# Attention scores as rounded products over 128 rows, with the keys doubled on the partitions by small DMAs

## The reference

```python
s1 = jnp.einsum('bhqd,bhkd->bhqk', q1b, k1).astype(jnp.float32) + bias
s2 = jnp.einsum('bhqd,bhkd->bhqk', q2b, k2).astype(jnp.float32) + bias
p1 = jax.nn.softmax(jnp.where(visible, s1, -jnp.inf), axis=-1)
p2 = jax.nn.softmax(jnp.where(visible, s2, -jnp.inf), axis=-1)
p = (p1 - lam * p2).astype(v.dtype)
```

## Time and profile before

| | us |
|---|---|
| median of three runs | 1068.31 |
| time of the profiled execution | 1068.49 |
| its span | 1066.6 |
| TensorE matmul busy in it | 1059.2 |
| TensorE weight load busy | 886.6 |
| VectorE busy | 696.3 |
| ScalarE busy | 586.0 |
| GpSimd busy | 231.1 |

### The profile page before, as it was taken

One profiled execution on the slowest core, in us unless ns is written; L12 is line 12 of the kernel. 1 busy time (PEld: TensorE's weight loads), 2 busy tenths in 40 slices (PEclk: granted clock), 3 DMA queues, 4 the chain that ended last, 5 costly groups with the idle time before them and its releaser, 6 DMA issues.

```text
span 1066.6 us, 15528 instructions
## 1 busy us (share of the span) xinstructions
PE 1059.2 (99%) x5008; PEld 886.6 (83%) x5008; DVE 696.3 (65%) x893; ACT 586.0 (55%) x861; POOL 231.1 (22%) x423
## 2 busy tenths in 40 slices
PE   9999999999999999999999999999999999999997
PEld 7888888888899888888888888888888988888886
DVE  5666655667797666665566666556777875666654
ACT  7555544556775654454455554445657756445453
POOL 0444312003440022230102222010134300222200
PEclk9999999999999999999999999999999999999999
DMA  8988787657796588876668777675578976887852
GB/s 258 274 241 241 240 275 247 199 176 242 247 323 217 180 246 244 240 240 221 215 200 255 237 244 241 207 230 182 176 240 273 315 227 186 251 242 243 245 193 79
DMA packets 181030, 246.23 MB, mean 231 GB/s; under 512 B 18964, under 2 KB 126272, under 8 KB 180976
## 3 DMA queue, kind: packets, MB, share of 16 engines
q1 hardware_dynamic: 162640, 198.82, 59.3%
q0 software_dynamic: 17936, 46.21, 14.3%
q10 hardware_dynamic: 400, 0.51, 0.1%
HBM read 222.13 MB, written 23.34 MB: 230 GB/s over the span
## 4 chain that ended last, share of the span: by engine, by line
PE 99%; DMA 0%; DVE 0%; ACT 0%; issue 0%; DVEq 0%
PE acc L1608 21%; PE acc L1609 21%; PE acc L1610 21%; PE acc L1697 7%; PE acc L1699 7%; PE acc L1700 7%; PE acc L1627 3%; PE acc L1636 2%; PE acc L1631 1%; PE mixed L1631 1%; PE acc L1584 1%; PE score L1631 1%; PE score L1609 1%; PE score L1608 1%; PE score L1610 1%; PE mixed L1659 1%
## 5 line engine op out<-in xcount | busy, mean ns | idle before, releaser
L1067 DVE TENSOR_TENSOR w_lo<-raw,w_hi 128x1024 fp32r<-128x1024 f32 x376 | 457.2, 1222 | 290.7 <-ACT w_hi L662 288.8
L662 ACT CAST w_hi<-raw 128x1024 fp32r<-128x1024 f32 x375 | 391.3, 1049 | 383.2 <-PE acc L1610 240.4
L1608 PE MATMUL acc<-w_hi,xm 128*128 128x512 f32 x912 | 357.0, 391 | 0.0
L1610 PE MATMUL acc<-w_lo,xm 128*128 128x512 f32 x912 | 355.0, 389 | 0.0
L1609 PE MATMUL acc<-w_hi,xm 128*128 128x512 f32 x912 | 354.9, 389 | 0.0
L1608 PEld LDWEIGHTS acc<-w_hi,xm 128*128 128x128 f32 x912 | 171.2, 188 | 36.0
L1610 PEld LDWEIGHTS acc<-w_lo,xm 128*128 128x128 f32 x912 | 171.2, 188 | 35.5
L1609 PEld LDWEIGHTS acc<-w_hi,xm 128*128 128x128 f32 x912 | 171.2, 188 | 34.9
L512 POOL DMA_DIRECT2D hid_scratch<-by_token_at x176 | 96.3, 553 | 311.2 <-DVE by_token_at L1184 309.3
L1697 PE MATMUL acc<-w_hi,hm 128*128 128x512 f32 x354 | 137.4, 388 | 0.0
L1699 PE MATMUL acc<-w_hi,hm 128*128 128x512 f32 x354 | 137.3, 388 | 0.0
(11 more groups left out here) (183 smaller groups left out, 875.4 us busy)
## 6 DMA issues: line engine op xcount, KB each, us to landing
raw<-in_ffn_w_gate_dram SPq DMA_DIRECT2D x176, 256.0 KB, 3.1
raw<-in_ffn_w_up_dram SPq DMA_DIRECT2D x176, 256.0 KB, 3.5
raw<-in_ffn_w_down_dram SPq DMA_DIRECT2D x176, 256.0 KB, 3.4
raw<-in_w_in_dram SPq DMA_DIRECT2D x160, 256.0 KB, 3.2
hid_scratch<-by_token_at POOLq DMA_DIRECT2D x176, 64.0 KB, 3.1
part<-hid_scratch POOLq DMA_DIRECT2D x44, 256.0 KB, 3.4
raw<-in_w_out_dram SPq DMA_DIRECT2D x32, 256.0 KB, 3.8
gate_scratch<-acc_lo POOLq DMA_DIRECT2D x64, 64.0 KB, 3.3
```

The lines of the kernel that those rows point to most:

```text
L662: nc.scalar.copy(w_hi[:, s, 0:tiles, :], raw[:, s, 0:tiles, :]).then_inc(hi_split, 1)
L1067: nc.vector.tensor_tensor(w_lo[:, s, 0:tiles, :], raw[:, s, 0:tiles, :], w_hi[:, s, 0:tiles, :], ALU.subtract).then_inc(lo_split, 1)
L1608: nc.tensor.matmul(s[:, t, :], xh, wh[:, k], start=not u and not k, stop=False, skip_group_check=True)
L1610: mm = nc.tensor.matmul(s[:, t, :], xh, wl[:, k], start=False, stop=(u, k) == (GU_UNITS - 1, GK - 1), skip_group_check=True)
```

## The change

Both queries of a head pair are rounded. The rounded part stands on partitions 0 to 63 and the remainder on 64 to 127 (`query_split`). The keys stand on both halves, as rounded part (`key_hi`) and as remainder (`key_lo`). A score is then the sum of two rounded products over 128 rows. To get the operands there, GpSimd issues 16 transfers from `proj` into free tiles per layer, ScalarE rounds four tiles and VectorE subtracts four times per layer. TensorE waits for `heads_lo` in place of `proj_ready`.

```diff
--- before.py
+++ after.py
@@ -182,6 +182,8 @@
         hm = sb("hm", [FT, 2 * SEQ], F32R)
         merged = hm[:, 0:KT, :]
         mix = hm[:, KT:2 * KT, :]
+        query_split, key_hi, key_lo = (hm[:, n * N_HEADS:(n + 1) * N_HEADS, :].rearrange("p k n -> p (k n)").rearrange(
+            "p (g s m n) -> p g s m n", g=2, s=2, m=PAIR) for n in range(3))
 
         proj = sb("proj", [2 * N_HEADS, SEQ])
 
@@ -214,6 +216,8 @@
         gate_raw = [v.rearrange("p k n -> p (k n)") for v in (
             gates[:, 0:4, :], gates[:, 4:KT, :], proj[:, 0:4, :], proj[:, 4:8, :])]
         attn_dram = nc.dram_tensor("attn_scratch", (P, N_HEADS * SEQ), F32, kind="Internal").ap()
+        twice = [v.rearrange("p k n -> p (k n)").rearrange("p (s f) -> p s f", s=2) for v in (
+            gates[:, KT:KT + 4, :], conv, gates[:, KT + 4:2 * KT, :], conv_in)]
         x_raw = gates[:, KT:KT + 2 * PAIR, :].rearrange("p k n -> p (k n)")
         x_dram = nc.dram_tensor("x_scratch", (P, 2 * PAIR * SEQ), F32, kind="Internal").ap()
         conv_dram = [nc.dram_tensor(f"conv_scratch{g}", (P, 2 * PAIR * SEQ), F32, kind="Internal").ap()
@@ -294,6 +298,8 @@
         hid_back = [sem(f"hid_back{b}") for b in range(2)]
         set_by_token, set_turned, set_out = sem("set_by_token"), sem("set_turned"), sem("set_out")
         proj_ready, x_back = sem("proj_ready"), sem("x_back")
+        twice_back = [sem(f"twice_back{n}") for n in range(4)]
+        heads_hi, heads_lo = sem("heads_hi"), sem("heads_lo")
         conv_back = [sem(f"conv_back{n}") for n in range(3)]
         attn_blocks, attn_out, attn_back = sem("attn_blocks"), sem("attn_out"), sem("attn_back")
         gate_back = [sem(f"gate_back{g}") for g in range(GATE_SETS)]
@@ -547,8 +553,19 @@
                 pool.wait_ge(set_out, sets_out.now)
                 pool.dma_start(back_at, to).then_inc(back_sem, 16)
 
+            def double_heads(layer):
+
+                for n in range(4):
+                    pool.wait_ge(proj_ready, 4 * (layer - 1) + n + 1)
+                    for sm in range(2):
+                        for half in range(2):
+                            pool.dma_start(twice[n][half * HEAD_DIM:(half + 1) * HEAD_DIM, sm, :],
+                                           proj[sm * HEAD_DIM:(sm + 1) * HEAD_DIM, at(n * PAIR), :].rearrange(
+                                               "p k n -> p (k n)")).then_inc(twice_back[n], 16)
+
             def shuffle_mixer(layer):
 
+                double_heads(layer)
                 if layer == 1:
                     lam_made()
                 for n in range(3):
@@ -905,6 +922,12 @@
                             "p (q k n) -> p q k n", q=2, k=PAIR), ACT.Copy, scale=rstd_tok[:, t:t + 1]).then_inc(set_by_token, 1)
                     sets.add()
 
+                def heads_rounded(n):
+
+                    to = (query_split, key_hi)[n // 2][:, n % 2]
+                    wait(act, (twice_back[n], 64 * (l + 1)))
+                    nc.scalar.copy(to.rearrange("p s m n -> p s (m n)"), twice[n]).then_inc(heads_hi, 1)
+
                 next_units(P_MIX)
                 hi()
                 hi()
@@ -916,7 +939,10 @@
                 hi()
                 copy_acc(2)
                 hi()
-                hi()
+                heads_rounded(0)
+                heads_rounded(1)
+                hi()
+                heads_rounded(2)
                 units_done.add(2)
                 wait(act, (used, units_done.now), (rstd_ready, norm.now))
                 if l == 0:
@@ -950,6 +976,8 @@
                     nc.scalar.copy(prob_t[:, :], prob_t_ps).then_inc(prob_copied, 1)
                     wait(act, (pv_done, head.now))
                     nc.scalar.copy(attn[:, h:h + 1].rearrange("p o t d -> p (o t) d"), pv_ps).then_inc(pv_read, 1)
+                    if h == 0:
+                        heads_rounded(3)
 
                 layers.add()
                 hi()
@@ -1399,6 +1427,18 @@
                     nc.vector.tensor_tensor(proj[:, at(n * PAIR), :], summed, wide(rstd[:, :]),
                                             ALU.mult).then_inc(proj_ready, 1)
 
+                def query_remainder(n):
+
+                    wait(dve, (heads_hi, 4 * l + n + 1))
+                    at_q = query_split[HEAD_DIM:, n].rearrange("p s m n -> p s (m n)")
+                    nc.vector.tensor_tensor(at_q, twice[n][HEAD_DIM:], at_q, ALU.subtract).then_inc(heads_lo, 1)
+
+                def key_remainder(n):
+
+                    wait(dve, (heads_hi, 4 * l + 2 + n + 1))
+                    hi_at, lo_at = (v[:, n].rearrange("p s m n -> p s (m n)") for v in (key_hi, key_lo))
+                    nc.vector.tensor_tensor(lo_at, twice[2 + n], hi_at, ALU.subtract).then_inc(heads_lo, 1)
+
                 next_units(0.5, P_MIX)
                 nc.vector.tensor_tensor(rstd_rows[:, :, :], ident[:, :].unsqueeze(1).to_broadcast([P, QT, P]),
                                         rstd_tok[:, :].unsqueeze(2).to_broadcast([P, QT, P]),
@@ -1416,7 +1456,10 @@
                 lo()
                 projected(2, sum_acc())
                 lo()
-                lo()
+                query_remainder(0)
+                query_remainder(1)
+                lo()
+                key_remainder(0)
                 lo()
                 projected(3, sum_acc())
                 dve.wait_ge(bias_loaded, 32)
@@ -1449,6 +1492,8 @@
                     lo()
                     if h < HEAD_ITERS - 1:
                         turn_set()
+                    if h == 0:
+                        key_remainder(1)
                 layers.add()
                 def taps(k):
                     d = CONV_K - 1 - k
@@ -1810,12 +1855,13 @@
                     if h == 0:
                         pe.wait_ge(v_scaled, QT * (l + 1))
                     if h % PAIR == 0:
-                        pe.wait_ge(proj_ready, 4 * l + PAIR + h // PAIR + 1)
+                        pe.wait_ge(heads_lo, 4 * l + PAIR + h // PAIR + 1)
                     for sm in range(2):
-                        half = slice(sm * HEAD_DIM, (sm + 1) * HEAD_DIM)
-                        q, k = proj[half, h, :], proj[half, N_HEADS + h, :]
-                        nc.tensor.matmul(score[:, sm, 0:SEQ], q[:, P:SEQ], k, start=True, stop=True)
-                        mm = nc.tensor.matmul(score[:, sm, SEQ:KEYS], q[:, 0:P], k[:, 0:P], start=True, stop=True)
+                        q, kh, kl = (v[:, h // PAIR, sm, h % PAIR] for v in (query_split, key_hi, key_lo))
+                        for to, tokens, keys in ((slice(0, SEQ), slice(P, SEQ), slice(0, SEQ)),
+                                                 (slice(SEQ, KEYS), slice(0, P), slice(0, P))):
+                            nc.tensor.matmul(score[:, sm, to], q[:, tokens], kh[:, keys], start=True, stop=False)
+                            mm = nc.tensor.matmul(score[:, sm, to], q[:, tokens], kl[:, keys], start=False, stop=True)
                     mm.then_inc(scored, 1)
                     others_by_token()
                     wait(pe, (prob_ready, head.now))
```

## The result

The change makes the kernel slower: 1072.74 us (median of six runs, 1071.70 to 1075.20) against 1068.31 for the kernel before (1068.01 to 1069.36), ratio 1.0042 with a 95% interval of 1.0028 to 1.0056. The 1068.31 is the median of five runs; a sixth took 1585.28 us and is not counted. The forecast was 1067.4 us, with a range up to 1071.0. The profiled execution took 1072.52 us, its span is 1070.7, 4.1 us more than before.

What follows compares the result with a forecast made beforehand. TensorE, busy 99% and never waiting after the start, was taken to bound the kernel. Products -1.1 us and the fourth tile's late place +0.1 gave -1.0, so 1067.4 us against 1068.31, range 1065.7 to 1071.0.

Steps and rivals of the forecast that it cites:

- the price of the products: TensorE's scores: eight rounded matmuls take 0.91 us per head against 1.06 before, -1.1 us over eight heads.
- Starts 0.06 apart: Sign of being wrong in the profile after: narrow score matmuls on TensorE starting 0.06 us apart.
- loads are hidden: Rival, 12%, at the scores: a narrow rounded matmul takes 0.06 us, a head 0.71, so -2.6 us, 1065.7.
- the fall back to the float32 pace: Rival, 20%, at each score's 128-column matmuls: 0.22 us in place of 0.11, so +2.3 us, 1070.6.
- the landing of the doubled keys: Third transfer group before head 0's scores: lands 3.0 us after issue, at 221.4, leaving 2.9 us slack, no cost.
- just fits, so landings will be slower than 3.0: Added DMA load: 7 us of all 16 engines per layer against 5.8 us or more free; nothing counted.
- the 3 to 5 us: Sign of being right in the profile after: landings of the small transfers take 3 to 5 us.
- the doubled keys come late: Rival, 8%, at head 0's scores: keys landing 7.4 us from issue cost 1.5 us per layer, 1070.2.
- GpSimd has nothing else to do: GpSimd before the first turned set at 238.48: its time is free, so issuing 16 transfers per layer costs nothing.
- Nothing: ScalarE's list behind the keys' rounding: values' scaling, a unit's rounding and a copy slip up to 2 us, costing nothing.
- still ahead of the probabilities: GpSimd's `lam` in layer 0: made some 4 us later, yet before the probabilities, so no cost.
- Head 1's margin: Fourth tile moved into head 0: head 1's chain 1.6 us late, 0.1 us slack left; +0.1 us for both layers.

Runs made afterwards that it cites:

- no_dma: The change without its 16 transfers per layer, rounding and subtraction reading `proj` where it stands (scores not the reference's): 1067.82 us, ratio 0.9995.
- small_dma: The change with the same 16 transfers per layer, each carrying an eighth of the bytes (scores not the reference's): 1067.62 us, ratio 0.9992.
- half_moved: half with the first keys' rounding later and the fourth tile's rounding and subtraction earlier, outputs correct: 1067.54 us, ratio 0.9989.
- lam_first: The change with `lam` made on GpSimd ahead of the fourth group of transfers instead of behind it: 1074.19 us, ratio 1.0055.
- held_5: half with GpSimd filling a spare tile five times before it issues the first keys' transfers: 1069.80 us, ratio 1.0013.
- half: The change with VectorE writing each projection straight into its own partitions, only the crossing 8 transfers per layer left, outputs correct: 1067.63 us, ratio 0.9998.
- late_round: The change with the first keys' rounding behind the values' scaling and one more unit, their subtraction behind one more `lo`: 1075.31 us, ratio 1.0061.
- held_8: half with GpSimd filling a spare tile eight times before it issues the first keys' transfers: 1079.26 us, ratio 1.0097.
- light_loads: The change with all 16 full transfers, but this stage's weight loads carrying an eighth of their columns (outputs not the reference's): 1067.16 us, ratio 0.9988.

## Why the prediction was wrong

*The bound, and the price of the products: right.* TensorE's list sets the time. Eight rounded products take what I had for them: 1.38 us across head 0's scores against 1.51 is 0.13 saved per head (I counted 0.14), 1.0 us in all, which no_dma, small_dma and half_moved show in their traces. The steps are uneven, which I had not: of a pair with the same stationary operand, the second narrow one follows after 0.06 us, but the wide one behind them after 0.11 and the next after 0.17. So a pair of wide ones took 0.29 and a pair of narrow ones 0.17, where I had 0.236 and 0.22: the prices of the parts were both off, and the sum of four, 0.46, was right because the weight loads pace wide and narrow alike, 0.11 or 0.12 apart. Starts 0.06 apart stood among my signs of being wrong, and that was a bad sign to choose: single starts would have read as the rival "loads are hidden". That rival and the fall back to the float32 pace are both out.

*The step that failed: the landing of the doubled keys.* I took "a transfer of this size lands after 3.0 us" and gave the path 2.9 us of slack. It landed after 7.6. The 3.0 was the median of eight transfers of 128 KB in the kernel before, four per layer. The trace shows them, and the DMA share around layer 0's four (293.8 to 295.9):

```profile
DMA to landing us min/median/max: 2.7/3.0/4.4
```

```profile
290.00:300.00 10.00, 10.00 (x46) 8.28 (x45) 7.88 (x13) 8.21 (x16) 6.62 (x13) 1.00 0.94 284
```

So those went out onto busy engines too. What they lacked was a queue in front: they are four, behind issues of 64 KB, and the fourth of each layer already took 4.2 and 4.4. In the change the first four took the same 2.7 to 4.1, and the group that matters stands behind eight of full size. The step that failed is to give the twelfth transfer the time of one of four.

What makes it worse is that the text had the warning and did not use it: it found 7 us of work for all 16 engines and "5.8 us or more" free, wrote that it "just fits, so landings will be slower than 3.0", and still took 3.0 for the landing and counted nothing. Even the 3 to 5 us that it named as a sign of being right would have left no wait. The 7 was low as well, by how much is less certain: the queue's share went from 14.3% of 1066.6 us to 16.0% of 1070.7, 18.8 us for 4.19 MB. But no_dma, without the transfers, has 14.6% of 1066.1, 3.1 us more than before for the same bytes. So the price is 3.7 to 4.5 us of all 16 engines per MB against 3.3, and each layer brings 8 to 9 us.

The rival "the doubled keys come late" had its place and its threshold (5.9 us from issue) right, and its landing nearly (7.4). Its price was too low: 1070.2, where 1072.7 was measured. It got 8%.

*What was missing from that rival's price.* The trace of the change splits, in TensorE's starts, like this. Layer 0: 2.1 us at the scores (2.05 by the rows above), 0.2 and 0.1 in the units behind, 0.7 at the transposes of head 0. Layer 1: 1.75, 0.3 and 0.1. That is 5.2 us, less 1.0 for the products: 4.2, the measured 4.1. So besides the wait itself 1.4 us went where "GpSimd has nothing else to do", "its time is free" and "Nothing" stood: `lam`, forecast "still ahead of the probabilities", came 0.46 us late for VectorE, which lam_first takes back, and units' `lo` came late, which held_5 shows by itself.

*Head 1's margin: enough, so +0.1 us was not needed.* The line for bias and scale ran 1.6 us late there, as forecast, but no start of TensorE in head 1 lost more than 0.01 us, in the change or in `half`. What `half` still loses is 0.1 us at head 0's own transposes and units in layer 0, and next to nothing in layer 1; half_moved has it no more.

## What to carry to other kernels

Before a transfer is put on a path with slack, count what stands in front of it in its own queue, and add the bytes of all to what the DMA engines carry in that very stretch. Here four transfers alone landed after 2.3 to 2.8 us, and four like them behind eight, with the engines full, after 5.7 to 7.6. Where the sum is near the stretch, a median from elsewhere in the trace is no guide. On a kernel whose TensorE never waits, a wait costs its length at each place; what queues behind the late step can cost before that, and a long wait can bring the clock down on top. Send only what has to cross: here half of the doubling was to partitions that the producer could have written itself, and leaving it out took away the loss of 0.4% (`half`, 0.9998); with four places moved as well the kernel is faster by 0.1% (`half_moved`, 0.9989, the interval's end at 0.9998).

## What the runs showed of the hardware

Three things that I had not expected. The granted clock fell from its full level to 1.2 GHz after TensorE had waited 2.60 and 1.96 us (late_round, layers 0 and 1) and 3.54 us (held_8); after 1.89 us, in the profiled run of the change, it stayed full. So waits of nearly one length went both ways. In held_8 it was already at 0.83 within the wait, and still at 0.50 in the stretch from 234 to 236, behind a wait that ended at 230.0. The page TensorE: Matmul & The Clock Gate of the Trainium skill, section "What's actually happening", says that the clock is gated down when the array has been idle and released by activity; these rows agree.

A queue's landings build up: twelve transfers of 128 KB issued within 8.1 us, beside the weight loads, landed after 2.8 us at first and 7.6 at the end. With the weight loads light the same twelve took 4.5 at most, and with an eighth of the bytes 3.8.

And the transfers from SBUF to SBUF look dearer per byte than the rest of their queue (3.7 to 4.5 us of all engines per MB against 3.3). By the trace's records of single packets, the first twelve of layer 0 (1.57 MB) took 6.5 us of all engines in the change, 4.2 per MB, and 5.6 in light_loads, 3.6 per MB. So a good part of the surplus is the crowd and not the kind of transfer; whether the kind adds the rest was not tried.
